# A hybrid streaming layer on one core: the sample tile's high and low halves in one TensorE operand, and two retention products moved into the sample's attention

## The reference, cut to what matters

```python
h = rmsnorm(x, norm_g)
rq, rk, rv, rg, aq, ak, av, ag, iq, ik, iw = jnp.split(h @ w_in, SPLIT_POINTS, axis=-1)
ro, new_ret = retention(rope(rq), rope(rk) * RET_HEAD_DIM ** -0.5, rv, ret_state)    # 4 heads of 128, chunks of 64
ro = rmsnorm(ro, ret_gn_g) * silu(rg)
ao = dsa_attend(...) * silu(ag)         # top 256 keys by the indexer, then softmax over them
y = rmsnorm(x + concat([ro, ao]) @ w_out, final_g)
```

## Time and profile before

| | us |
|---|---|
| median of 3 runs | 892.48 |
| lowest, highest | 889.42, 894.42 |
| profiled execution, own time | 888.84 |
| its span in the profile | 887.3 |
| TensorE busy | 796.1 |
| VectorE busy | 478.8 |
| ScalarE busy | 330.0 |
| GpSimd busy | 168.2 |

### The profile page before, as it was taken

The page is one execution under the profiler, slowest core; times in us unless marked ns, Lnnn a source line. Parts: engine busy times, 40 slices in busy tenths (PEclk is TensorE's granted clock), DMA queues, the critical chain, the costliest instruction groups (busy, mean ns, idle before and its releaser), DMA issues.

```text
span 887.3 us, 12344 instructions
## 1 busy us (share of the span) xinstructions
PE 796.1 (90%) x4197; PEld 667.7 (75%) x4197; DVE 478.8 (54%) x1182; ACT 330.0 (37%) x748; POOL 168.2 (19%) x361
## 2 busy tenths in 40 slices
PE   1898978898989999979699999999998999999984
PEld 1787867776777868858678888888886888888873
DVE  3643576778777887779753433333356432333322
ACT  4644455566557575666461111111235200000000
POOL 0333223131222213010111222222221111111101
PEclk9998979899999999899889999999999999999998
DMA  7522012212103002104553212121475533333321
GB/s 217 185 84 82 29 42 74 78 38 76 40 20 130 9 12 65 36 0 118 150 141 103 90 66 65 65 65 65 148 218 185 163 100 104 109 106 103 110 70 35
DMA packets 40447, 79.79 MB, mean 90 GB/s; under 512 B 12673, under 2 KB 14097, under 8 KB 39121
## 3 DMA queue, kind: packets, MB, share of 16 engines
q1 hardware_dynamic: 33072, 59.03, 21.4%
q0 software_dynamic: 6448, 19.36, 6.7%
q10 hardware_dynamic: 880, 0.83, 0.3%
HBM read 58.67 MB, written 20.53 MB: 89 GB/s over the span
## 4 chain that ended last, share of the span: by engine, by line
PE 62%; DVE 15%; issue 7%; ACT 7%; DMA 6%; POOL 2%; ACTq 0%; SPq 0%; DVEq 0%; POOLq 0%
PE bank L841 46%; PE bank L966 4%; DMA xT<-turned_x 3%; DVE probs L1574 3%; PE bank L955 2%; DVE work L1473 2%; PE bank L856 2%; ACT pT L1201 1%; PE bank L949 1%; DVE idx L1454 1%; PE bank L903 1%; DVE w_lo L1365 1%; PE bank L950 1%; PE bank L904 1%; DMA stage<-in_w_out 1%
## 5 line engine op out<-in xcount | busy, mean ns | idle before, releaser
L841 PE MATMUL bank<-w_hi,xT 128*128 128x512 f32 (+1 forms) x1152 | 375.9, 396 | 10.5 <-DVE xT L1401 4.4
L841 PEld LDWEIGHTS bank<-w_hi,xT 128*128 128x128 f32 x1152 | 218.6, 192 | 61.4 <-DMA xT<-turned_x 5.7
L841 PE MATMUL bank<-w_lo,xT 128*128 128x512 f32 (+1 forms) x576 | 224.8, 390 | 0.0
L841 PEld LDWEIGHTS bank<-w_lo,xT 128*128 128x128 f32 x576 | 111.1, 193 | 19.1
L966 PE MATMUL bank<-v_sb,pT 128*128 128x64 f32 x648 | 92.0, 282 | 7.1 <-ACT pT L1201 6.5
L966 PEld LDWEIGHTS bank<-v_sb,pT 128*128 128x128 f32 x648 | 85.4, 201 | 13.7 <-ACT pT L1201 12.7
L955 PE MATMUL bank<-ident,probs 128*128 128x128 f32 x324 | 55.4, 283 | 21.9 <-ACT probs L1190 21.9
L1201 ACT COPY pT<-bank 128x512 f32<-128x512 f32 (+3 forms) x104 | 49.2, 487 | 63.5 <-PE bank L955 62.6
L1190 ACT ACTIVATE probs<-probs,low 128x128 f32<-128x128 f32 (+8 forms) x68 | 54.4, 801 | 40.1 <-DVE low L1574 40.0
L955 PEld LDWEIGHTS bank<-ident,probs 128*128 128x128 f32 x324 | 39.5, 148 | 30.5 <-ACT probs L1190 28.5
L841 PE MATMUL bank<-w_hi,mT_hi 128*128 128x512 f32 x144 | 57.7, 400 | 2.6 <-DVE y_row L1754 2.6
(11 more groups left out here) (189 smaller groups left out, 1175.5 us busy)
## 6 DMA issues: line engine op xcount, KB each, us to landing
xT<-turned_x SPq DMA_DIRECT2D x34, 512.0 KB, 4.1
stage<-in_w_in SPq DMA_DIRECT2D x40, 256.0 KB, 3.0
turned_x<-xT SPq DMA_DIRECT2D x9, 1024.0 KB, 5.4
y_row<-in_x_prompt SPq DMA_DIRECT2D x16, 256.0 KB, 5.4
stage<-in_w_out SPq DMA_DIRECT2D x16, 256.0 KB, 3.1
out<-y_row POOLq DMA_DIRECT2D x16, 256.0 KB, 2.4
xin<-in_x_prompt SPq DMA_DIRECT2D x14, 256.0 KB, 3.7
early<-in_w_in SPq DMA_DIRECT2D x3, 1024.0 KB, 7.4
```

The lines of the kernel that those rows point to most:

```text
L841: mm = pe.matmul(out, (lo if which == 2 else hi)[:, k, :], (w_lo if which == 1 else w_hi)[slot][:, k, 0:width], start=(i == 0), stop=(i == ...
```

## The change

1. **The sample's operand.** `xT` and the turned mixed rows are laid out as (k, high/low, rows) instead of (high/low, k, rows). For the sample, the second 64 columns of the high part and the first 64 of the low part lie side by side and are taken as one stationary operand of 128 columns (`product_sample`). It is multiplied by high and by low weights: 16 matmuls instead of 24. Rows 0 to 63 of the bank then hold the product of the high parts, rows 64 to 127 that of the low parts. ScalarE copies the lower block of rows to partitions 0 to 63 in SBUF (`lift`), VectorE adds it (`unite`, or in `output` a second addition). This holds for seven products: q, k, v of the sample in stage R, `rg`, `ag`, `y0`, `y1` in stage O. The result is in 64 rows only; its store is done twice. TensorE's and ScalarE's loops have one turn less, and the last turn is written out.
2. **The moved products.** The q product of tile 0 of stage R stands ahead of the sample's attention on TensorE; its k product is cut into two halves of 12 matmuls, which stand behind heads 1 and 2 in the sample's attention. VectorE rotates q behind head 3's weight splits, and k right behind the attention, before the `rg` splits. To free banks 5 and 6 for them, the sample's attention goes round five banks, and banks of stages R and O are exchanged.
3. **Loads of x.** A half of `xT` is now one contiguous piece in each partition (and in HBM) instead of two.

```diff
+RETAINED = {(SAMPLE, 1): [("rk", 0)], (SAMPLE, 2): [("rk", 1)], (SAMPLE, 3): [("angles", 0)]}
...
+        if (t, h) in RETAINED:
+            order += [("between", *item) for item in RETAINED[t, h]]
...
-        xT = sb("xT", [P, 2, KD, P], F32R)
-        xT_hi, xT_lo = xT[:, 0], xT[:, 1]
-        xT_raw = xT[:].bitcast(F32).rearrange("p a k n -> p a (k n)")
...
+        mT = sb("mT", [P, KD, 2, P], F32R, at=at)
+        mT_hi, mT_lo = mT[:, :, 0, :], mT[:, :, 1, :]
...
+            among = NB - 3 if t == SAMPLE else NB - 1
...
+        R_BANK = {"q": 5, "k": 6, "v": 2, "kv": 3, "out": 4, "turn_q": 0, "turn_k": 1, "scores": 7}
...
+        O_BANK = {"rg": 5, "ag": 6, "y1": 2, "turn0": 0, "turn1": 1, "y0": 7}
...
-                    s = slice(half * BW, (half + 1) * BW)
-                    sp.dma_start(xT_raw[:, :, s],
-                                 xT_mem[bass.ds(t * P, P), :, s]).then_inc(xT_in[half], 16)
+                    s = slice(half * D, (half + 1) * D)
+                    sp.dma_start(xT_raw[:, s], xT_mem[bass.ds(t * P, P), s]).then_inc(xT_in[half], 16)
...
+            def product_sample(key, slot, rows, x=None, last=False):
+
+                wait_free(pe, key)
+                for k in range(KD):
+                    if x and k % 4 == 0:
+                        if x[0] == "spill":
+                            pe.wait_ge(xT_in[k // 4], 16 * (x[1] + 1))
+                        else:
+                            wait_drained(pe, (f"{x[0]}{k // 4}", *x[1:]))
+                    both = rows[:, k].rearrange("p a n -> p (a n)")[:, DEC:DEC + P]
+                    for which, w in enumerate((w_hi, w_lo)):
+                        mm = pe.matmul(of(key)[:], both, w[slot][:, k, :], start=(k == 0 and which == 0),
+                                       stop=(k == KD - 1 and which == 1))
+                    if last and k == KD // 2 - 1:
+                        mm.then_inc(xT_half_used, 1)
+                mm.then_inc(*fills(key))
...
+            def project_r(name, t, first=False, part=(0, PRODUCTS)):
+                if isinstance(t, int) and t == SAMPLE:
+                    product_sample((name, "R", t), SLOT[f"r{name}"], xT,
+                                   ("spill", spill_no("R", t)) if name == "q" else None, name == "v")
+                    return
+                project(name, f"r{name}", "R", t, first, part, x=("spill", spill_no("R", t)) if name == "q" else None,
+                        last=(name == "v"))
...
+                elif name == "rk":
+                    project_r("k", 0, True, (t * PRODUCTS // 2, (t + 1) * PRODUCTS // 2))
...
                 turn_queries("turn_aq", t, aq_row)
+            project_r("q", 0, True)
             attend(SAMPLE)
...
-            for name in "qkv":
-                project_r(name, 0, True)
+            project_r("v", 0, True)
             retain_tile(0, True)
-            with pe.Fori(1, NT) as t:
+            with pe.Fori(1, NT - 1) as t:
                 retain_tile(t)
+            retain_tile(NT - 1)
 
...
+                    if not gates:
+                        product_sample((f"y{half}", "O", t), SLOT[f"wo{half}"], mT,
+                                       ("turn", "O", t) if half == 0 else None)
+                        continue
...
+            def lift(key, dst):
+
+                wait_filled(act, key)
+                if united_no[key] > 1:
+                    act.wait_ge(united, united_no[key] - 1)
+                act.copy(dst[0:DEC, :], of(key)[DEC:P, :]).then_inc(lifted, 1)
...
             turned(NT - 1)
+            lift(("q", "R", SAMPLE), gate[:, 0:BW])
             for k in range(3):
                 round_w("ag", k)
+            lift(("k", "R", SAMPLE), gate[:, 0:BW])
             square(NT - 1)
+            lift(("v", "R", SAMPLE), gate[:, 0:BW])
+            act.wait_ge(united, united_no["v", "R", SAMPLE])
             retained(SAMPLE)
             for k in range(3, 6):
...
-            with act.Fori(1, NT) as t:
+            with act.Fori(1, NT - 1) as t:
                 hi_mixed(t)
                 gates(t + 1)
+            hi_mixed(NT - 1)
+            for name in ("rg", "ag"):
+                lift((name, "O", SAMPLE), rtmp[:].rearrange("p h d -> p (h d)"))
+            act.wait_ge(united, united_no["ag", "O", SAMPLE])
+            gates(SAMPLE)
             wait_filled(act, ("y1", "O", NT - 1))
             hi_mixed(SAMPLE)
+            for half in range(2):
+                lift((f"y{half}", "O", SAMPLE), (rq_row, rk_row)[half][:].rearrange("p h d -> p (h d)"))
...
+                elif name == "angles":
+                    rotate_q(t)
...
+            def unite(key, part):
+
+                dve.wait_ge(lifted, united_no[key])
+                dve.tensor_tensor(of(key)[0:DEC, :], of(key)[0:DEC, :], part[0:DEC, :], ALU.add).then_inc(united, 1)
+                dve.wait_ge(united, united_no[key])
...
+                if isinstance(t, int) and t == SAMPLE:
+                    unite(key, gate[:, 0:BW])
...
+            rotate_k(0)
             dve.memset(state[:], 0.0).then_inc(state_zero, 1)
             for k in range(3):
                 split_w("rg", k)
             dve.wait_ge(state_zero, 1)
-            rotate_q(0)
-            rotate_k(0)
             dve.wait_ge(r_early_in, R_EARLY)
...
             retain(NT - 1, state, P)
+            unite(("v", "R", SAMPLE), gate[:, 0:BW])
             for k in range(3, 6):
                 split_w("ag", k)
             decay_scores(SAMPLE, dec_s)
...
+                    if row is gate:
+                        dve.wait_ge(lifted, united_no[key])
                     dve.tensor_tensor(row[:, s], of(key)[:], row[:, s], ALU.add).then_inc(*drains(key))
                     wait_drained(dve, key)
+                    if row is gate:
+                        dve.tensor_tensor(row[0:DEC, s], row[0:DEC, s],
+                                          (rq_row, rk_row)[half_][0:DEC].rearrange("p h d -> p (h d)"), ALU.add)\
+                           .then_inc(united, 1)
+                        dve.wait_ge(united, united_no[key])
                     ins = half_stats(row, half_)
...
+            for name in ("rg", "ag"):
+                unite((name, "O", SAMPLE), rtmp[:].rearrange("p h d -> p (h d)"))
             mix(SAMPLE)
             lo_mixed(SAMPLE)
...
+                if isinstance(t, int) and t == SAMPLE:
+                    for half in range(2):
+                        pool.dma_start(ret_mem[t * P + half * DEC:t * P + (half + 1) * DEC, :],
+                                       ro[0:DEC].rearrange("p h d -> p (h d)")).then_inc(ro_stored, 16)
+                    return
```

More of the change, by code:

```diff
@@ L457, in take_attention @@
                     for key in cached_banks(*step[1:]):
-                        take(key)
-                elif step[0] == "between" and step[1] != "weights":
+                        take(key, among=among)
+                elif step[0] == "between" and step[1] not in ("weights", "rk", "angles"):
                     take((step[1], "A", step[2]))
                 elif step[0] in ("score", "turn"):
-                    take((*step, t))
+                    take((*step, t), among=among)
             take(("attended", t), NB - 1)
@@ L847, in product @@
                     mm.then_inc(*fills(key))
+            def product_sample(key, slot, rows, x=None, last=False):
[13 more added lines that the diff above has]
+                mm.then_inc(*fills(key))
             def project(name, w, phase, t, first, part=(0, PRODUCTS), x=None, last=False, of_x=xT):
[L850 removed]
+                product((name, phase, t), SLOT[w], WIDTH[w], of_x[:, :, 0, :], of_x[:, :, 1, :], w if first else None, part, x,
                         last)
@@ L1033, in retain @@
                 ahead[2]()
-            def project_r(name, t, first=False):
-                project(name, f"r{name}", "R", t, first, x=("spill", spill_no("R", t)) if name == "q" else None,
-                        last=(name == "v"))
             def retain_tile(t, first=False):
@@ L1340, in hi_mixed @@
                 for half in range(2):
-                    hi((f"turn{half}", "O", t), mT_hi[:, 4 * half:4 * half + 4, :].rearrange("p k n -> p (k n)"))
+                    key = (f"turn{half}", "O", t)
+                    rows = of(key)[:].rearrange("p (k n) -> p k n", n=P)
+                    dst = mT_hi[:, 4 * half:4 * half + 4, :]
+                    if isinstance(t, int) and t == SAMPLE:
+                        hi(key, dst[:, :, DEC:P], rows[:, :, 0:DEC])
+                    else:
+                        hi(key, dst, rows)
             square(SAMPLE)
```

108 lines of the change are left out of this document (61 added, 47 removed).

## The result

| | before | after |
|---|---|---|
| median (lowest to highest), 20 runs each | 893.19 (888.54 to 896.06) | 887.62 (882.78 to 892.28) |
| ratio, 95% interval | | 0.9943 (0.9928 to 0.9958) |
| profiled span | 887.3 | 886.3 |

The change makes the kernel faster by 5.6 us, 0.6%. The direction was forecast, the size was not: the forecast was 11.6 us, to 880.0, and the range ended at 887.0.

What follows compares the result with a forecast made beforehand. TensorE, busy 90% of the span, was taken to bound the kernel. Output stage 6.7, retention's operand 2.2, moved products 2.1 and layout 0.6 summed to 11.6 us; 880.0 us was named, range 874 to 887.

Steps and rivals of the forecast that it cites:

- output stage: Output stage: 32 fewer matmuls and a shorter stop, less a longer tail behind the last product; gain 6.7 us (5.5 to 8.0).
- retention's operand: Retention stage: 24 fewer matmuls, followed through the sample's copy of v and the weight loads; gain 2.2 us (0.5 to 4.0).
- moved products: Around the sample's attention: q and k of tile 0 fill TensorE's stops; net gain 2.1 us (-2.5 to 6.5).
- layout: Loads of x: each half in one 4 KB piece per partition; gain 0.6 us over seven tiles (0 to 1.2).
- the clock stays what it is: Output stage, before the last two products: the stop shrinks from 2.60 to 1.95 us, but the clock doesn't change.
- the k product ends 16 matmuls earlier (3.7 us): End of retention: the sample's k product ends 3.7 us earlier, its rotation 2.4 us earlier after copy and addition.
- the sum for v: End of retention: VectorE's 0.7 us sum queues behind tile 7's retention, so v's copy starts only 1.0 us earlier.
- I take 5.0: Second tile's x load: issued at 469.0, lands after 5.0 us, at 474.0 instead of 477.8.
- rival B: Moved work paid back in full: x lands no earlier, clock low behind the new stop; gain 5.5 to 7.5; chance 0.16.
- rival C: Sums eat the retention tail: v's copy later since ScalarE or VectorE serve the sums late; gain about 8; chance 0.08.
- rival F: Little gain: rivals B and C together with a longer attention; gain 0 to 4.4 us; chance 0.07.
- The two rules: Trainium skill: 0.216 us per matmul makes the sum 11.1; line rate from 512 bytes makes the layout nothing, sum 11.0.

Runs made afterwards that it cites:

- e3: Changed kernel with the second tile's x loaded ahead of gate weights 3 to 5 on SP's queue; 883.69 us, ratio 0.9906.
- e9: e3 with two one-column multiplications on GpSimd, one behind the stores of attended rows, one behind the loads of constants; 887.62 us, ratio 0.9925.
- e13: e3 with a one-column multiplication on GpSimd between its wait for the attended rows and their first store; 876.85 us, ratio 0.9839.
- e2: Changed kernel with the sample's operand in the output stage alone, its q, k, v back at 24 matmuls; 885.83 us, ratio 0.9934.
- e8: Changed kernel without the moved products and with the sample's operand in the output stage alone, new x layout kept; 885.92 us, ratio 0.9930.
- e11: e5 with the retention's q, k, v products of the sample back at 24 matmuls; 876.24 us, ratio 0.9811.
- e6: e3 with the sample's attended rows stored in pieces of 1 KB instead of 256 bytes, columns reordered; 881.70 us, ratio 0.9875.
- e10: e3 with GpSimd's wait for the two early constants moved ahead of the stores of the sample's attended rows; 887.65 us, ratio 0.9923.
- e7: Changed kernel with VectorE's sum for the sample's v ahead of the end of tile 7's retention; 887.15 us, ratio 0.9938.
- e5: e3 with decayed keys and tile 1's angles ahead of the sample's stores and the constants' loads on GpSimd; 875.77 us, ratio 0.9808.
- e15: e1 with the x load of tile 1 ahead of gate weights 3 to 5; 885.79 us, ratio 0.9939.
- e4: Changed kernel with GpSimd's three loads of constants held until the second tile's x has landed; 884.63 us, ratio 0.9909.
- e1: Changed kernel with q and k of tile 0 back behind the sample's attention; 886.15 us, ratio 0.9933.

## Why the forecast was wrong

By the profile of after, the four terms of the sum missed by +1.5 (output stage), -4.6 (retention's operand), -3.8 (moved products) and 0 us (layout).

**Output stage: 6.7 forecast, 8.2 in the profile** (196.50 less 186.80, less 1.46 behind the last matmul). The terms were right: the chain of after shows the tail as forecast, and the last 32 matmuls:

```profile
863.21 0.61 DVE y_row L1841
...
863.86 7.74 PE bank L872 x32
...
871.62 0.59 ACT rk_row L1327
...
872.31 0.70 DVE gate L1841
...
873.03 0.70 DVE gate L1844
```

TensorE stood 1.85 us instead of 2.60 (1.95 forecast). The step that was off is "the clock stays what it is": here it stayed full behind the shorter stop. But it did so only in some profiles. From the first to the last start of the 32 matmuls it is 7.3 us in nine kernels and 8.9 in seven, with the same products. In e3's window the clock is low again:

```profile
858.00:862.00 4.00, 3.88 (x11) 3.04 (x12) 3.11 (x9) 0.00 (x0) 0.56 (x1) 0.66 0.01 4
```

So the term is 8.2 or 6.7, with the clock up or down. (e9 and e13 have 6.0: each of their output tiles takes 0.08 us longer, for which no row gives a reason.)

**Retention's operand: 2.2 forecast, a loss of 2.4 in the profile of after.** Two steps failed. First, "the k product ends 16 matmuls earlier (3.7 us)". Eight of them are the q product's, and these are eaten by a wait for the second half of x. Only the other eight count, and the copy and the sum take most of that back. Measured from the scores of tile 7, the k rotation of VectorE is 0.5 us earlier (648.61 in after, 644.29 in the earlier trace rows), not 2.4. Second, the sum for v was rightly seen queued behind the end of tile 7's retention, but with nothing gained ahead of it the copy of v is later, 15.83 us behind the scores of tile 7 instead of 15.0. Rows of TensorE, VectorE and ScalarE, and of the chain:

```profile
639.49 0.50 PE L872 MATMUL bank<-w_hi,xT 128*128 128x512 f32 x1 [1.63 <-DMA xT<-turned_x]
```

```profile
648.61 0.69 DVE L1644 TENSOR_TENSOR rk_row<-bank,rot_r 128x512 f32<-128x512 f32 x1
...
655.53 1.13 DVE L1765 SCALAR_TENSOR_TENSOR ro<-bank,rstd,gn_t 128x128 f32<-128x128 f32 x4 [1.14 <-POOL rstd L1889]
656.58 0.68 DVE L1632 TENSOR_TENSOR bank<-bank,gate 64x512 f32<-64x512 f32 x1
```

```profile
657.29 0.58 ACT L1334 COPY rv_row<-bank 128x512 f32<-128x512 f32 x1 [4.02 <-DVE bank L1632]
```

```profile
661.59 7.80 DMA stage<-in_w_out
```

The load of output weights takes 7.80 us, not less than 6.31. The stop before the gate product, 2.84 us in the earlier trace rows, is 6.77: the products ahead of it got shorter, the chain didn't.

```profile
677.26 0.79 PE L853 MATMUL bank<-w_hi,xT 128*128 128x512 f32 x1 [6.77 <-ACT gate L1392]
```

The kernels with 24 matmuls here (e2, e8, e11) need 63.4 to 63.7 us for the stretch, the nine others with the sum for v late 63.65 to 65.08, 64.3 in the mean (e6 and e10 stand apart with 66.1 and 66.3). Before has 62.72. So some 0.8 us of the mean loss of 1.6 is the operand's. Cut at the scores of tile 7, the stretch shows the rest. Up to them it is 21.8 us in before and in after, but 22.7 in e2, e8 and e11: with 24 matmuls too, TensorE now waits for x inside the sample's q product (0.33 and 0.65 us in e8; not at all in before), since its second half lands 4.7 us after the issue instead of 3.7. Behind them e2, e8 and e11 need 40.7 to 41.0, like before (40.9), after 43.3, and the nine 42.5 in the mean. So the shorter products win back the 0.9 us of that wait, and the sums then cost 1.7. Why the second half lands later in every changed kernel stays open.

**Moved products: +2.1 forecast, -1.7 in the profile.** Right: q hides in the stop, the clock behind it is full, the attention ends 0.94 us later (1.0 forecast), and the load of x is the next wait. Wrong is "I take 5.0": it landed after 8.6, behind the gate weights of its own queue and beside the constants. Tile 1 began 1.1 us earlier, not 3.9, behind a stop of 10.58 and not 7. And the loss of the clock was 2.9 us, not 1.8: the q product took 8.4 us, not 5.6, since most of its 24 matmuls ran at the lower level. That size is one execution's: in e2 and e7 it took 7.1 and 7.4, a loss of 1.5 and 1.8 as forecast, and the scores of tile 0 come 0.1 and 0.2 us later than before, not 1.7. So the landing is the step that failed in all three, the size of the clock's loss in one. Nearest is rival B (the load no earlier, the clock low behind the new stop), which had 0.16. The measured gain of 5.6 lies in its 5.5 to 7.5 (the time, 887.6, lies beyond its 887, since the median of before was 893.19 here and not 892.48), but in part by luck: the retention's operand lost too (rival C's late copy of v), and the output stage gained 1.5 more in the profile. B and C together were priced as rival F, at 0 to 4.4 and a chance of 0.07, too low a gain.

**Layout: 0.6 forecast.** From the scores of tile 0 to those of tile 6 it is 131.19 us before; in the twelve kernels where no late angles disturb it, after among them, it is 130.5 to 131.2, 0.35 less in the mean, or 0.4 for seven tiles. This is within the spread.

**The two rules.** The 96 matmuls of a tile still take 22.31 us in the chain of after, 0.232 each. The 0.216 that the Trainium skill gives ("TensorE: Matmul & The Clock Gate", section "Wait — 56ns, not 53.3ns?") is not seen here. That pieces above 512 bytes make no difference ("DMA: Bandwidth & Descriptors", section "Specifications") fits the layout's small term as well as 0.6 does; no run tells them apart.

**Size of it all.** With x issued early and GpSimd's hold avoided, the scores of tile 0 come after 38.58 us in e5 instead of 50.09: the moved products can be worth 11.5 us (10.85 against the 49.43 of e15, which has the early x and no move), and the change itself got none of it.

## What to carry to other kernels

Work that is moved off the critical path pays only if all that the next step waits for moves too: here a load's place in SP's queue and an order on GpSimd stood between -1.7 and +11.5 us; the load alone kept some 4 of its 13 us, the order alone none. A transfer that starts right behind other loads of its queue and beside another queue's isn't priced by the median of its undisturbed rows: 3.6 us became 8.6. And a saving counts at the wait that ends the stage: follow it instruction by instruction, and ask at each product whether its input is there.

## What was not expected of the hardware

- GpSimd's arithmetic starts 8 to 12 us late where it goes from a wait of 26 to 30 us straight to DMA issues (12.04 in after, 11.34 in e2, 10.22 in e3, 8.14 in e4, 10.01 in e6, 11.39 in e7, 9.68 in e8, 9.20 in e9, 11.46 in e10). One multiplication of one column (0.20 us) ahead of the issues removes this (e13). The profile names it "issue"; its cause is open.
- GpSimd's queue, mostly with loads of constants, took 75% of the DMA engines' time for 0.37 MB in 4 us. A load of x beside it, and behind three loads on its own queue, needed 8.6 us; with the constants held back 6.4 (e4), with neither 3.7 (before) and 3.2 (e1).
- Behind a stop of 1.85 us with the same work around it, the clock stayed at its upper level in the profiles of nine kernels and fell to the lower in those of seven, 1.5 us apart.
